# Query weights of all eight PEER heads kept on chip for both tiles, a gather ring of seven slots, and a pair's weights made behind its second dot

## What is computed

```python
def peer_ffn(x, w_q, sub_keys, u, v):
    q = (x @ w_q).reshape(B, S, PEER_HEADS, 2, PEER_DK // 2)      # 8 heads, 2 x 128
    s = jnp.einsum('bshcd,cnd->bshcn', q, sub_keys)               # 2 x 128 keys
    sv, si = lax.top_k(s, PEER_TOPK)                              # 16 of each
    ...
    best_s, pos = lax.top_k(cand_s, PEER_TOPK)                    # 16 of 16 x 16
    e_idx = jnp.take_along_axis(cand_i, pos, axis=-1)
    gate = jax.nn.softmax(best_s, axis=-1)
    ...
    hid = jax.nn.gelu(jnp.einsum('td,ted->te', xt, u[et]))        # a row of u per expert
    return jnp.einsum('te,ted->td', gt * hid, v[et])              # a row of v per expert

for layer in range(2):
    h = layer_norm(DN_ALPHA * h + mixer(h), ...)
    h = layer_norm(DN_ALPHA * h + peer_ffn(h), ...)
```

## Time and profile before

| | us |
|---|---|
| median of 3 runs | 1594.32 (1591.54 to 1594.63) |
| profiled execution | 1593.75 |
| its span, first to last instruction | 1591.9 |
| PE busy | 1351.2 |
| DVE busy | 1064.4 |
| ACT busy | 488.0 |
| POOL busy | 494.5 |
| bytes by DMA | 601.20 MB, of them 536.90 MB gathers |
| mean granted clock of PE | 0.969 |

### The profile page before, as it was taken

One profiled execution on the slowest core, in us unless ns is written; L12 is line 12 of the kernel. 1 busy time (PEld: TensorE's weight loads), 2 busy tenths in 40 slices (PEclk: granted clock), 3 DMA queues, 4 the chain that ended last, 5 costly groups with the idle time before them and its releaser, 6 DMA issues.

```text
span 1591.9 us, 16214 instructions
## 1 busy us (share of the span) xinstructions
PE 1351.2 (85%) x5046; PEld 733.5 (46%) x5046; DVE 1064.4 (67%) x2835; ACT 488.0 (31%) x1274; POOL 494.5 (31%) x524
## 2 busy tenths in 40 slices
PE   7999888888887888789889879988778988887877
PEld 7888534433354454444446634444334443333322
DVE  1127876778867877676653587777875876776765
ACT  1122342334323332223334233343332322222222
POOL 0003333334333333333320133343333333333331
PEclk9999998989998999999999989999999999999999
DMA  9528999999999999999993499999999999999996
GB/s 353 188 102 322 399 408 421 409 414 411 409 410 403 422 417 422 418 421 385 406 388 106 171 416 420 408 411 419 407 390 420 414 402 421 420 421 422 421 421 268
DMA packets 92821, 601.20 MB, mean 378 GB/s; under 512 B 10432, under 2 KB 12864, under 8 KB 26560
## 3 DMA queue, kind: packets, MB, share of 16 engines
q0 software_dynamic: 73728, 536.90, 82.2%
q1 hardware_dynamic: 19008, 63.28, 10.5%
HBM read 599.09 MB, written 1.05 MB: 377 GB/s over the span
## 4 chain that ended last, share of the span: by engine, by line
PE 37%; DMA 33%; DVE 22%; issue 3%; ACT 3%; DVEq 2%; POOL 0%; SPq 0%; POOLq 0%
DMA uv<-in_peer_uv_dram,expert 32%; PE y L638 19%; DVE uv L1621 11%; PE spare L536 3%; PE y L500 3%; PE px L353 2%; PE y L378 2%; ACT diag L1228 1%; DVE key_idx L1511 1%; DVE key_left L1503 1%; DVE key_idx L1505 1%; PE spare L395 1%; DVE wts L1627 1%; DVE key_top L1500 1%; DVE pos L1528 1%
## 5 line engine op out<-in xcount | busy, mean ns | idle before, releaser
L638 PE MATMUL y<-uv,diag 128*128 128x512 f32 x1888 | 912.9, 623 | 167.7 <-ACT diag L1228 166.9
L1621 DVE CUSTOM_DVE_ANT_0 uv<-px,uv 128x1024 f32<-128x1024 f32 x512 | 617.5, 1220 | 305.8 <-DMA uv<-in_peer_uv_dram,expert 299.6
L1073 POOL DMA_INDIRECT uv<-in_peer_uv_dram,expert x512 | 491.0, 959 | 1064.0 <-PE y L638 838.4
L638 PEld LDWEIGHTS y<-uv,diag 128*128 128x128 f32 x1888 | 349.5, 197 | 610.1 <-issue 341.6
L1228 ACT ACTIVATE diag<-ident,wts 128x128 f32<-128x128 f32 x472 | 166.3, 394 | 440.1 <-DVE wts L1627 430.9
L1220 ACT ACTIVATE act_hid<-hid 128x2 f32<-128x2 f32 x260 | 52.9, 203 | 482.4 <-DVE hid L1621 482.0
L1220 ACT ACT_TABLE_LOAD x54 | 69.3, 1283 | 1.0
L477 PE MATMUL spare<-ident,probs 128*128 128x128 f32 x96 | 16.9, 302 | 39.2 <-DVE probs L1448 35.8
L1640 DVE SCALAR_TENSOR_TENSOR vsum<-uv,wts,vsum 128x1024 f32<-128x1024 f32 x37 | 47.5, 1284 | 3.8 <-issue 0.5
L1627 DVE TENSOR_TENSOR wts<-act_hid,gate 128x2 f32<-128x2 f32 x260 | 40.6, 156 | 12.5 <-ACT act_hid L1220 12.4
L1621 DVE DVE_READ_ACCUMULATOR2_ANT hid<- 128x1 f32 x512 | 42.3, 83 | 0.0
(11 more groups left out here) (268 smaller groups left out, 1272.6 us busy)
## 6 DMA issues: line engine op xcount, KB each, us to landing
uv<-in_peer_uv_dram,expert POOLq DMA_INDIRECT x512, 10.8
wb_rows<-in_peer_w_q_dram SPq DMA_DIRECT2D x16, 512.0 KB, 8.7
uv<-in_na_w_dram SPq DMA_DIRECT2D x11, 512.0 KB, 9.9
wb_rows<-in_na_w_out_dram SPq DMA_DIRECT2D x8, 512.0 KB, 9.0
uv<-in_mla_w_out_dram SPq DMA_DIRECT2D x8, 512.0 KB, 10.7
wb_rows<-in_mla_w_out_dram SPq DMA_DIRECT2D x8, 512.0 KB, 7.8
bias<-in_na_bias_dram SPq DMA_DIRECT2D x16, 160.0 KB, 7.5
w_vu<-in_na_w_dram SPq DMA_DIRECT2D x4, 512.0 KB, 8.6
```

The source lines that it names most:

```text
L638: last = T.matmul(Y[t][:, c, :], diag[:, n % RING, :], uv[:, n % RING, 1, c * 512:(c + 1) * 512], start=False, stop=(k == TOPK - 1 and g % ...
L1073: pool.indirect_dma_start(uv[:, n % RING, :, :].rearrange("p h d -> p (h d)"), None, uv_table, bass.IndirectOffsetOnAxis(ap=expert[:, g, k ...
L1621: V_.tensor_tensor_reduce(out=rows, in0=px[:, :, :], in1=rows, scale=1.0, scalar=0.0, op0=ALU.mult, op1=ALU.add, accum_out=hid[:, k:k + 1] ...
```

## The change

The ring gets seven slots, and `diag` with it. `wb_rows` becomes a single row, `out_rows`. The room goes to `w_q6` and `w_q7`, so that the query weights of all eight heads are loaded once per layer. In the neighbourhood stage `w_q7` first carries the K and Q weights of head pair 7, as `w_qn` does for pair 5. On DVE the weights of every pair now come right behind its second dot.

```diff
-RING = 8
+RING = 7
-WB = 3
-KEPT = 6
...
-        wb_rows = sb("wb_rows", [P, WB, D])
+        out_rows = sb("out_rows", [P, D])
...
+        w_q6 = sb("w_q6", [P, 2, D])
+        w_q7 = sb("w_q7", [P, 2, D])
...
+        kept += [[w[:, c, :] for c in range(2)] for w in (w_q6, w_q7)]
-        pair5 = kept[4]
+        whole_pair = {5: kept[4], 7: kept[7]}
...
+        def last_row_in(slot):
+            return [n for n in range(STEPS - RING, STEPS) if n % RING == slot][0]
...
             def queries(layer, g, c, b):
                 t = g // PH
-                if is_kept(layer, g):
-                    pe.wait_ge(s_kept[g % PH], 32 * (layer + 1))
-                    w = kept[g % PH][c].rearrange("p (k n) -> p k n", k=DK)
-                else:
-                    w = side_item("q", layer, g, c).rearrange("p (k n) -> p k n", k=DK)
+                pe.wait_ge(s_kept[g % PH], 32 * (layer + 1))
+                w = kept[g % PH][c].rearrange("p (k n) -> p k n", k=DK)
...
             def line_load(part, j, src):
...
-                    sp.wait_ge(s_acc, acc_no(STEPS - RING + slot + 1))
+                    sp.wait_ge(s_acc, acc_no(last_row_in(slot) + 1))
...
             def side_load(src, *name):
...
+                if n == 1:
+                    sp.wait_ge(s_full[rest_bank(6)], job["rest", 6])
+                elif n > 1:
+                    sp.wait_ge(s_y, name[1] - PAIRS * (n == PAIRS + 1))
+                sp.dma_start(out_rows[:, :], src).then_inc(s_side, 16)
...
-                if 3 <= j < 5:
-                    kept_load(0, j - 3)
+                if 3 <= j < 6:
+                    kept_load(0, (0, 1, 6)[j - 3])
...
                 for j in range(PAIRS):
                     n = pair_no(layer, 1, j)
-                    if j + 3 < PH:
-                        side_load(peer_w_q[layer, j + 3, 0], "q", layer, j + 3, 0)
                     side_load(w_o[j], "O", n)
-                    if j + 3 < PH:
-                        side_load(peer_w_q[layer, j + 3, 1], "q", layer, j + 3, 1)
+                    if layer == 0 and j == 0:
+                        sp.wait_ge(s_full[rest_bank(PAIRS - 1)], job["rest", PAIRS - 1])
+                        kept_load(0, 7)
...
-                for g in range(PH, GROUPS):
-                    for c in range(2):
-                        side_load(peer_w_q[layer, g % PH, c], "q", layer, g, c)
...
+            for h in (6, 7):
+                sp.wait_ge(s_full[6], job["q", 0, PH + h])
                 kept_load(1, h)
             layer_loads(1)
...
-                    pool.wait_ge(s_acc, acc_no(STEPS - RING + 6))
+                    pool.wait_ge(s_acc, acc_no(last_row_in(5) + 1))
...
-                        elif n == 7:
+                        elif n == RING - 1:
                             pool.wait_ge(s_k6, 1)
...
                     for k in range(TOPK):
                         dot(layer, g, k)
-                        if g % PH == PH - 1 and k >= TOPK - 4:
...
-                        elif k % SUB == 0 and (g, k) not in ((0, 0), (PH, 0)):
-                            if k:
-                                weights(layer, g, k // SUB - 1)
-                            else:
-                                weights(layer, g - 1, SUBS - 1)
+                        for s, (first, end) in enumerate(subs(g)):
+                            if k == end - 1:
+                                weights(layer, g, s)
                         side(layer, g * TOPK + k)
```

More of the change, by code:

```diff
@@ L191, in program @@
         s_k6 = sem("rest_of_keys6_projected")
-        s_pair5 = [sem(f"pair5_weights_landed{i}") for i in range(2)]
-        s_wb = [sem(f"side_item_landed{i}") for i in range(WB)]
+        s_pair = {j: [sem(f"pair{j}_weights_landed{i}") for i in range(2)] for j in whole_pair}
+        s_side = sem("side_rows_landed")
         s_bias = [sem(f"bias_landed{i}") for i in range(BIAS_RING)]
-        s_kept = [sem(f"kept_queries_landed{h}") for h in range(KEPT)]
+        s_kept = [sem(f"kept_queries_landed{h}") for h in range(PH)]
         s_full = {b: sem(f"bank{b}_filled") for b in B}
@@ L255, in program @@
         line_no = {}
-        aside = [("Q", 6), ("K", 7), ("Q", 7)]
         for j in range(PAIRS):
             for part in "KQ":
-                if (part, j) not in aside and j < 5:
+                if j < 5:
                     line_no[part, j] = len(line_no)
@@ L274, in program @@
         through_no["O", PAIRS - 1] = len(through_no)
[L276 to L279 removed]
+        side_no = {("Q", 6): 0}
         for layer in range(LAYERS):
[L281 to L284 removed]
             for j in range(PAIRS):
[L286 to L287 removed]
                 side_no["O", pair_no(layer, 1, j)] = len(side_no)
[L289 to L294 removed]
         fills = {b: 0 for b in B}
@@ L920, in side_load @@
             def side_load(src, *name):
-                if name[0] == "q" and is_kept(name[1], name[2]):
-                    return
                 n = side_no[name]
-                if n >= WB:
-                    before = [other for other, no in side_no.items() if no == n - WB][0]
-                    if before in aside:
-                        sp.wait_ge(s_full[rest_bank(before[1])], job["rest", before[1]])
-                    elif before[0] == "O":
-                        sp.wait_ge(s_y, before[1] + 1)
-                    elif before[3] == 0:
-                        sp.wait_ge(s_q0, before[1] * GROUPS + before[2] + 1)
-                    else:
-                        layer, g = before[1], before[2]
-                        sp.wait_ge(s_full[7 if 3 <= g < PH else 6], job["q", layer, g])
-                sp.dma_start(wb_rows[:, n % WB, :], src).then_inc(s_wb[n % WB], 16)
+                if n == 1:
[3 more added lines that the diff above has]
+                sp.dma_start(out_rows[:, :], src).then_inc(s_side, 16)
             def kept_load(layer, h):
@@ L1011, in layer_loads @@
                              [(w_qr[:, :, :, :], mla_qr, s_qrs), (w_qs[:, :, :, :], mla_qs, s_qrs)]]
-                    for h in range(KEPT):
+                    for h in range(len(loads)):
                         sp.wait_ge(s_full[6], job["q", 0, PH + h])
```

41 lines of the change are left out of this document (12 added, 29 removed).

## The result

| | before | after |
|---|---|---|
| median of 4 runs, us | 1592.93 (1591.41 to 1594.63) | 1624.20 (1618.05 to 1628.73) |
| profiled execution, us | 1593.75 | 1627.56 |
| its span, us, and granted TensorE clock | 1591.9, 0.969 | 1625.7, 0.944 |

The changed kernel is slower: the ratio is 1.0185, with a 95% interval of 1.0154 to 1.0215. The forecast was 1600 us, with a range up to 1614. The side was right and the size was not: +6 was forecast and +31 came (+29.5 by the ratio), and the time lies 10 us above the range.

What follows compares the result with a forecast made beforehand. The prediction took the DMA engines to bound the gather stages, at a ceiling of 421 GB/s. From 1593.75 us, -12.4 - 2.4 + 20.9 = +6.1 gave 1599.9, said as 1600 us, with a range of 1583 to 1614.

Steps and rivals of the forecast that it cites:

- ten loads fewer: In the gather stages, ten weight loads for heads 6 and 7 drop out, 1.245 us of DMA time each: -12.4 us.
- the boundary: At the end of layer 0, output-weight loads wait for the last adds, so the last two dots come sooner: -2.4 us.
- DVE's wait for the Gelu: Some 250 pairs make DVE wait behind the second dot, 68 us, hidden in its waits for gathers except where DVE is behind.
- the slot, without anything given back: In the gather ring, one slot less costs a whole row of 2.49 us in each of 14 dips: 35 us.
- the part that earlier weights give back: Weights behind the second dot come 0.78 us earlier in a burst, shrinking the cover lost per dip from 2.49 to 1.71.
- the ring's term: Seven slots with earlier weights lose 1.71 us in 13 dips and gain 1.30 in one: +20.9 us.
- the 14 dips of before: Neighbouring 10 us slices of the gather stages at 402 GB/s or less, where DVE or PE fell behind with side work.
- the bytes don't matter: Rival: where PE is the late engine fewer loads free nothing, 7.5 us of the gain go; 1607 us, chance 0.05.
- The rival of the lock: DVE and ACT lock together, DVE standing through ACT's table reloads before Gelus; 1609 us, chance 0.08.
- The cover holds: Rival: bursts still leave gathers queued nearly everywhere, so the shorter ring costs only 5 us; 1584 us, chance 0.29.
- they cancel: Rival: each dip costs half of 1.71 us, 12 us in all; 1591 us, chance 0.20.
- The signs that I had named: 4.2 MB less, last layer 0 dots at 2.49, 60 to 80 us Gelu waits, more slow slices mainly in first tiles.

Runs made afterwards that it cites:

- e3: The kernel before with a ring of seven slots instead of eight and nothing else; 1631.79 us, ratio 1.0250.
- e2: The changed kernel with the weights back behind the next pair's first dot; 1624.15 us, ratio 1.0197.
- e4: The kernel before with a ring of seven and weights behind the second dot, heads 6 and 7 still loaded per tile; 1633.10 us, ratio 1.0252.
- e13: e3 with eight zero matmuls ahead of PE's wait for each attention pair of tile 1; 1627.28 us, ratio 1.0208.
- e15: e2 with eight zero matmuls ahead of PE's wait for each attention pair of tile 1; 1614.57 us, ratio 1.0118.
- e10: The kernel before with weights behind the second dot, and PE's attention, norm and latent transposes and first tile 1 queries put later; 1588.17 us, ratio 0.9957.
- e11: e10 with all eight heads kept and one output-weight row, ring still eight, room from shared buffers and six diag slots; 1572.21 us, ratio 0.9858 to the kernel before.
- e1: The kernel before with only the weights moved behind the second dot, ring of eight, six heads kept; 1591.09 us, ratio 0.9991.
- e12: The changed kernel with twelve zero matmuls ahead of PE's wait for each attention pair of tile 1; 1609.55 us, ratio 1.0092 to the kernel before.
- e9: The changed kernel with PE's attention transposes in tile 1 two rows later and one key-score projection at row 13; 1605.61 us, ratio 1.0055 to the kernel before.
- e7: The changed kernel with a ring of eight, head 7 using head 6's query weights, twelve loads fewer than before; 1575.80 us, ratio 0.9892 to the kernel before.
- e5: e1 with PE's attention transposes in tile 1 two rows later and one key-score projection at row 14; 1589.81 us, ratio 0.9985.

## Why the prediction was right in its side and wrong in its size

| term | forecast us | measured us | by |
|---|---|---|---|
| ten loads fewer | -12.4 | -8, -11 and -14 at seven slots; -16 at eight | e3 to e2, e4 to changed, e13 to e15; e10 to e11 |
| the boundary | -2.4 | -2.5, contained in the slot's +40 | the last dots of layer 0 |
| DVE's wait for the Gelu | 0, 68 of wait | 0, 71.8 of wait | e1 |
| the slot, without anything given back | 35 as the upper end | +40, with the boundary's gain in it | e3 |
| the part that earlier weights give back | -14 | 0, net of what they cost | e1; e3 to e4; e2 to changed |
| sum | +6.1 | +29, with the -11 | the changed kernel's ratio gives +29.5 |

**The step that failed is the ring's term, +20.9, in both of its factors.** The first is the count. I took the 14 dips of before and asked what each would cost more. But a ring shorter by one slot also makes dips where there were none: 25 in e3 and 31 in the changed kernel, where the same count gives 15 before. The trace before could have warned me: gathers land 10.8 us after their issue in the median and 5.5 at least, so in the median case the cover was about two rows of 2.49 us, and I took one of them away. Even one whole row in all 14 dips, my upper end of 35 us, is less than the 40 that e3 measured (its interval reaches down to 33; e4, with the earlier weights, has 36 to 44, and both already contain the boundary's gain).

The second is the price per dip. I let the earlier weights shrink each row's 2.49 us to 1.71. Three pairs of kernels show nothing of that; in each the interval excludes 14 us. The prediction had the reason in its own words: "in most PE is the late engine and has no use for earlier weights". It used that sentence against a gain over all dips and gave the 0.78 us a dip all the same. With the full 2.49 in all 14 its own sum would have come to about 1614. The weights do come earlier, and PE does use them; it then waits 22 to 29 us longer at the 16 transposes, and at seven slots filling that wait is worth 15 us (e12). The prediction named this very place, in the sentence on PE's waits for DVE's side work, but only as one where nothing is gained ("don't move"). The wait moved from 35.8 to 70.5 us. The right question was what else changes when an engine arrives early: its pause grows. Without the pause (e9) the changed kernel is 0.55%, 9 us, above the one before, by the medians on the same chip 11 us, which is close to the forecast. That closeness is in part luck: the forecast left the new dips out and counted on a gain from the earlier weights that no run shows.

**The bytes.** The 4.2 MB went as forecast, and so did their value at eight slots (1.3 us a load in e7, 1.245 forecast). At seven slots 8, 11 and 14 us came of the 12.4, and all three intervals contain the 12.4. So that bytes are worth less in a short ring, as the rival "the bytes don't matter" has it, is not shown, and it is not excluded either.

**The boundary.** In the last two steps of layer 0 the changed kernel gains 2.5 us on the one before (-2.4 forecast), and no dot is 3.6 us late there. It comes with the ring of seven: e3 and e4 have it, and the kernels with eight slots don't.

**The Gelu.** 247 waits, 71.8 us, within the forecast 60 to 80, and no time lost by them at eight slots. The rival of the lock, 1609 us, would have been the nearest in size and is wrong in its cause: the same waits stand in e1, the longest of them 2.5 us.

**The other rivals.** "The cover holds" and "they cancel" are out; they had 5 and 12 us for the slot with earlier weights, and e4 measured 40. With the first goes the use made of the Trainium skill's formula for a DMA ("DMA: Bandwidth & Descriptors", section "Anatomy of one DMA"): 4.4 us for a gather by that page spoke for cover to spare, and the shortest gather in e3 took 5.4.

**The signs that I had named** came out as follows: the bytes, the boundary and the Gelu as forecast; DVE's wait for gathers shorter by 47 us and not 60 to 80; more slices under 402 GB/s in the first tiles, yes; hardly any in the last, no.

**What stays open.** Of the slot's 40 us the filled pauses of e13 took back 7, not clear of the noise; how the rest divides over PE's and DVE's bursts was not measured. Nobody ran e3 with late transposes, which would say how much of the slot's price is the pause at the transposes, or e9 with the weights behind the next dot, which would price the earlier weights without the pause. In e12 the filling also moves the moments at which PE reaches the later rows, so its 15 us are the clock and that shift together. Theory E, dips from DVE's bursts, can still hold for a part.

## What to carry to other kernels

Before a ring gives up a slot, don't count the dips that are there: compare the time in the queue (landing less the shortest landing) with a slot's time, and expect new dips if it is only two slots. Here ten loads fewer bought 8 to 16 us and the slot that made room for them cost 40, so look for the room of kept data in buffers that are never alive together before taking it from the ring. When an edit makes data ready earlier for an in-order engine, look for the places where that engine waits for somebody else, and move them too: in this kernel it arrived early and paused there.

## What the runs showed of the hardware that was not expected

A pause of PE costs more than its length: after 5.24 us of waiting the next twelve matmuls took 7.76 us instead of 5.32, at a granted clock of 0.73 and 0.59 in the two windows of 5 us. Matmuls with zeros in the wait, twelve at each of 16 places, went with 0.98 instead of 0.92 in the first tile and made the whole kernel 15 us faster, though PE was given more to do. The same filling at eight slots gave 0.17%, with intervals that overlap. The likely reason, which was argued and not tested by itself, is that with eight slots nobody waits for PE behind the pause. Taking the pauses away did not bring the clock back by itself: in e5 the lower level lasted as long as in e1.
